# Odd layer's order at the heads' seams: k's rotation behind the output additions, y's transposes moved between products

## The reference

```python
def retention_mixer(h, pos, w_in, w_out):
    q, k, v, z = _split(h @ w_in, ODD_SPLITS)              # 4 heads: q, k 256 wide, v, z 512 wide
    q = xpos_rotate(q.reshape(qk_shape), pos)
    k = xpos_rotate(k.reshape(qk_shape), pos) * (RET_QK_DIM ** -0.5)
    v = v.reshape(bsz, s, RET_HEADS, RET_V_DIM)
    o = rms_norm(multiscale_retention(q, k, v)).reshape(bsz, s, ODD_MIX)
    return (jax.nn.silu(z) * o) @ w_out                    # y @ w_out, added to x
```

## Time and profile before

| | |
|---|---|
| median of 3 runs | 1869.29 us (1869.04 to 1871.68) |
| profiled execution | 1863.59 us, its span 1861.8 us |
| PE busy | 1779.9 us, 96% of the span |
| DVE, ACT, POOL busy | 657.0, 445.0, 239.3 us |
| mean granted clock of TensorE | 0.981 |

### The profile page before, as it was taken

How to read it: one execution, slowest core, us unless ns; L and a number is a source line. 1 busy time by engine, 2 the same in 40 slices (tenths; PEclk the granted TensorE clock), 3 DMA queues, 4 the chain that set the end, 5 groups by cost and what they waited for, 6 DMA issues and landing times. The chain is left out here.

```text
span 1861.8 us, 23173 instructions
## 1 busy us (share of the span) xinstructions
PE 1779.9 (96%) x9225; PEld 1131.5 (61%) x9225; DVE 657.0 (35%) x1141; ACT 445.0 (24%) x845; POOL 239.3 (13%) x154
## 2 busy tenths in 40 slices
PE   7999777999999999999999999999999999999998
PEld 7778776864545454544777877777854444545453
DVE  3666665343233332323413113130342323233333
ACT  4355535221111111111332132313321111111110
POOL 2521001100000000000243244234100000000000
PEclk9989898999999999999999999999999999999999
DMA  8310020279999999999122212122189999999996
GB/s 191 91 45 1 1 92 2 91 274 409 409 409 410 410 410 410 410 409 399 55 91 91 89 47 90 65 72 91 52 341 409 409 409 410 410 410 409 410 410 251
DMA packets 140953, 460.44 MB, mean 247 GB/s; under 512 B 5329, under 2 KB 31153, under 8 KB 139985
## 3 DMA queue, kind: packets, MB, share of 16 engines
q1 hardware_dynamic: 140080, 457.07, 63.2%
q0 software_dynamic: 800, 2.35, 1.0%
HBM read 457.30 MB, written 2.10 MB: 247 GB/s over the span
## 5 line engine op out<-in xcount | busy, mean ns | idle before, releaser
L1524 PE MATMUL bank<-ring,SCR 128*64 128x512 f32 x2048 | 448.3, 593 | 1.1 <-DVE SCR L1504 0.9
L153 PE MATMUL bank<-ring_r 128*128 128x512 f32 (+1 forms) x1152 | 355.2, 389 | 1.4 <-ACT SCR L507 1.4
L1524 PEld LDWEIGHTS bank<-ring,SCR 128*64 128x64 f32 x2048 | 152.7, 137 | 290.3 <-issue 284.9
L153 PEld LDWEIGHTS bank<-ring_r 128*128 128x128 f32 x1152 | 216.4, 190 | 47.4 <-issue 3.1
L1535 PE MATMUL bank<-ring,SCR 128*64 128x512 f32 x1024 | 226.8, 595 | 0.0
L1812 DVE TENSOR_TENSOR X<-X,bank 128x512 f32<-128x512 f32 x256 | 164.0, 681 | 99.7 <-PE bank L1542 99.3
L1962 POOL TENSOR_TENSOR ring_r<-ring,ring_r 128x1024 fp32r<-128x1024 f32 x60 | 145.0, 2449 | 253.0 <-ACT ring_r L1955 253.0
L1542 PE MATMUL bank<-SCR_r 128*128 128x512 f32 x512 | 153.4, 422 | 5.2 <-DVE SCR_r L1551 4.5
L1535 PEld LDWEIGHTS bank<-ring,SCR 128*64 128x64 f32 x1024 | 70.8, 137 | 132.1 <-issue 128.5
L1554 DVE SCALAR_TENSOR_TENSOR SCR<-SCR,bank 128x512 f32<-128x512 f32 x32 | 23.9, 748 | 359.4 <-PE bank L1524 359.4
L153 PE MATMUL bank<-ring_r,SCR_r 128*128 128x512 f32 x576 | 139.8, 401 | 10.2 <-DVE X L2167 10.2
(11 more groups left out here) (399 smaller groups left out, 1778.7 us busy)
## 6 DMA issues: line engine op xcount, KB each, us to landing
ring<-in_w_gate_dram SPq DMA_DIRECT2D x64, 2048.0 KB, 15.1
ring<-in_w_up_dram SPq DMA_DIRECT2D x64, 2048.0 KB, 18.4
ring<-in_w_down_dram SPq DMA_DIRECT2D x64, 2048.0 KB, 14.7
ring<-in_w_in_odd_dram SPq DMA_DIRECT2D x8, 2048.0 KB, 8.7
ring<-in_w_in_even_dram SPq DMA_DIRECT2D x16, 512.0 KB, 6.5
ring<-in_w_in_odd_dram SPq DMA_DIRECT2D x8, 1024.0 KB, 8.1
ring<-in_w_out_odd_dram SPq DMA_DIRECT2D x4, 2048.0 KB, 7.7
ring<-in_w_out_even_dram SPq DMA_DIRECT2D x2, 2048.0 KB, 10.4
```

What stands on the lines that cost most here:

```text
L153: mm = pe.matmul(out, lhs[a], rhs[b], start=(first and i == 0), stop=(last and i == 2))
L1524: mm = pe.matmul(bank[SLOTS * u:SLOTS * u + SLOTS, :], x_tile(k, u), w[u][:, k, :], start=(k == 0), stop=(k == KT - 1))
```

## The change

It touches the order of instructions on three engines, at the three seams. No instruction is added or removed.

```diff
--- before.py
+++ after.py
@@ -1967,10 +1967,12 @@
             left.append({"qk": ("r_qk", 2 * h + 2), "v": ("r_v", NT * (h + 1)), "z": ("r_z", NT * (h + 1)), "out": ("r_out", 8 * (h + 1))}[name])
         left = [(sg(a), b) for a, b in left]
 
-        def ret_qk_pe(pe, h):
+        def ret_qk_pe(pe, h, between=()):
             j, c, w = odd_chunk("qk", h)
             w = [a.rearrange("p (k s n) -> p k s n", k=KT, s=2) for a in w]
             for s in range(2):
+                for t in between if s else ():
+                    ret_yt_pe(pe, h - 1, t)
                 for par in range(2):
                     if h:
                         pe.wait_ge(sg("r_o_out"), NT * (h - 1) + 2 * s + par + 1)
@@ -2013,10 +2015,11 @@
                 if h < RH - 1:
                     for t in range(1, NT):
                         ret_z_pe(pe, h, t)
-                    ret_qk_pe(pe, h + 1)
-                    for t in range(NT):
-                        ret_yt_pe(pe, h, t)
+                    ret_qk_pe(pe, h + 1, (0, 1))
                     for n in range(8):
+                        if n == 2:
+                            ret_yt_pe(pe, h, 2)
+                            ret_yt_pe(pe, h, 3)
                         ret_out_pe(pe, h, n)
                 else:
                     ret_z_pe(pe, h, 1)
@@ -2104,8 +2107,8 @@
                     split_act(act, at("out", h))
                 for t in range(NT) if h < RH - 1 else range(1, NT):
                     yt_out(h, t)
-                if h < RH - 1:
-                    split_act(act, at("v", h + 1))
+                    if h < RH - 1 and t == 1:
+                        split_act(act, at("v", h + 1))
 
         def ret_pool(pool, step):
             at = lambda name, h: odd_at[name, h][0]
@@ -2155,12 +2158,13 @@
                         yt_lower(h, 0)
                 if h < RH - 1:
                     rotate(h + 1, both[0:1])
-                for t in range(NT) if h < RH - 1 else range(1, NT):
+                for t in range(2) if h < RH - 1 else range(1, NT):
                     yt_lower(h, t)
-                if h < RH - 1:
-                    rotate(h + 1, both[1:2])
                 for n in range(8):
                     t, half = n // 2, n % 2
+                    if h < RH - 1 and n == 2:
+                        yt_lower(h, 2)
+                        yt_lower(h, 3)
                     dve.wait_ge(sg("r_out"), 8 * h + n + 1)
                     xs = X[:, t, half * 512:(half + 1) * 512]
                     dve.wait_ge(resid, R_MOE0 + 8 * h)
@@ -2169,6 +2173,8 @@
                         if n == 1:
                             router_gain(dve, 1)
                         router_dve(dve, 1, n)
+                if h < RH - 1:
+                    rotate(h + 1, both[1:2])
 
 
         released = {c_kv: (sg("a_proj"), 4), c_q: (sg("a_proj"), 8)}
```

## The result

| | before | after |
|---|---|---|
| median | 1869.26 us (1869.04 to 1871.68, 4 runs) | 1850.49 us (1849.36 to 1853.49, 4 runs) |
| ratio | | 0.9908 [0.9893, 0.9924] |
| span of the profiled execution | 1861.8 us | 1847.5 us |

A forecast was written before the change was run, and what follows sets the result against it. TensorE was taken to bound the kernel, so time comes only from its waits and lower clock at three seams. 12.9 + 3.2 = 16.1 us gives 1847.5 us profiled, 1853.1 us for the median; range 1849.8 to 1858.4.

The forecast's parts named there:

- The two waits: At each seam TensorE idles 1.11 us for tile 0's lower part and 2.74 us for half tile 0's addition; both go.
- The seam's 12.9 us: From transposes to half tile 2's addition, 14.81 us against 10.52 of work: 4.29 us per seam, 12.9 over three.
- The clock's 3.2 us: Clock falls behind the first and third seams' idle time, 1.65 and 1.60 us, vanish with that idle time.
- k's rotation: Moved behind addition 7 on VectorE, it still ends before the next head's scores, with 14.7 us of slack.
- The copy of tile 2: On ScalarE behind four v casts taking 3.90 us, the copy still has some 2.1 us of slack.
- From the transposes of tile 2 to half tile 4: The 2.22 us chain of transpose, copy and difference is covered by transposes and products, with 4.3 us of slack.
- The remainder of the program moves up as a whole.: Second expert layer loads are released by TensorE's work behind the last seam, so everything after it starts earlier.
- rival 1: The waits go but the clock falls come elsewhere: gain 12.9 us, 1856.4 us; chance 0.14.
- the 5.7 us: Runs' median 1869.29 us lies this far above the profiled execution; it carries over, turning 1847.5 into 1853.1 us.
- Rival 2: The timed runs had a clock fall at all three seams: gain 17.8 us, 1851.5 us; chance 0.13.
- The port rule: Beside GpSimd the moved rotation stays slow, additions and differences are untouched; otherwise only 1.4 us of gain left.
- rival 4: Transpose-only stretches, two per seam, let the clock fall: six falls of 1.65 us, gain 6.2 us, 1863.1 us; chance 0.02.

The follow-up runs named there:

- e1: Kernel before with only k's rotation moved behind the additions on VectorE, transposes left together: ratio 0.9929 [0.9915, 0.9943].
- e2: Changed kernel with k's rotation put back ahead of the additions, so only transposes, copies and lower parts move: ratio 0.9931 [0.9917, 0.9944].
- e3: Kernel before plus ten useless products in TensorE's idle time ahead of half tile 2: median 1864.27 us against 1867.54, ratio 0.998.
- r1: Kernel before, unedited, run and profiled a second time: median 1867.51 us against 1867.54, ratio 0.9999 [0.999, 1.0008].
- e8: Changed kernel with nine useless casts ahead of v's casts on ScalarE: 1871.81 us in one execution, against 1866.52 for the kernel before.
- e5: Changed kernel with the four products of k's rotation done eleven times, rotation 29.0 us: median 1878.39 us, ratio 1.0063 against the kernel before.
- e4: Changed kernel with the four products of k's rotation done seven times, rotation 18.9 us: ratio 0.9902 [0.9887, 0.9917] against the kernel before.
- second pair: Second profiles of either kernel, both unedited: spans 1865.6 us before and 1848.2 us after.
- first pair: First profiles of the kernel before and the changed kernel: spans 1861.8 us and 1847.5 us.
- e6: Changed kernel with additions 0 and 1 ahead of tile 3's lower part in the last head: median 1845.89 us against the changed kernel's 1850.07, ratio 0.9887.
- first comparison: Kernel before against changed kernel, four runs each: medians 1869.26 and 1850.49 us, ratio 0.9908.
- r2: Changed kernel, unedited, run and profiled a second time: median 1850.07 us against 1867.16 for the kernel before, ratio 0.9906 [0.9893, 0.992].

## Why the prediction was right, point by point

**The two waits end, and nothing takes their place.** Right: the view of waits is empty over the seams. By e1 and e2 the waits were not two independent costs: either edit alone gives about two thirds of the whole. The prediction took the seam as a whole, from transposes to addition 2, and that is why its sum is right.

**The seam's 12.9 us.** Measured 107.14 − 102.66 = 4.48 us a seam, 13.4 in all. Two terms for the work that is left were off, in opposite directions. The 1.08 us for eight transposes had been read from transposes that started behind a wait; within running work they take 0.87 (1001.39 to 1002.26), so the work was put 0.42 us a seam too high. The changes between product and transposes were costed at nothing; the first matmul behind transposes takes 0.33 us instead of 0.23 (1002.26 to 1002.59), twice a seam, so the work was put 0.2 us too low. With both put right the forecast is 4.51 us a seam.

**The clock's 3.2 us.** Right in cause, and right in size for the profiled execution. The two falls cost 3.28 us by the marks (16.72 − 13.44), and e3, which has all the waits but fills one, gains 3.3. That equal waits may or may not bring a fall was right as well. Over all profiles of this study, by the length of TensorE's idle time in the odd layer's mixer:

| idle time | places | falls behind it |
|---|---|---|
| 1.1 us (transposes) | 12 (before, r1, e1, e3) | 0 |
| 1.4 us (e2) | 3 | 0 |
| 2.0 us (last head) | 11 | 7 |
| 2.7 us (before, r1) | 6 | 4 |
| 4.3 us (e8) | 3 | 3 |
| 7.9 us (e5) | 3 | 3 |

The length of one idle time does not settle it alone: in the router's work behind the mixer, where the longest is 0.93 us, 8 of the 12 profiles have a fall. What brings those was not tested.

**The slacks.** k's rotation: 14.7 us predicted, 14.6 measured (1043.48 to 1058.09), and e4 and e5 lie on the two sides of it. The copy of tile 2: 2.1 predicted, 1.97 measured. From the transposes of tile 2 to half tile 4: 4.3 predicted, and this step was wrong. It followed transpose, copy and lower part alone, and forgot that addition 2 is queued behind the lower parts of tiles 2 and 3 and frees the bank of half tile 4. In e8 the copies start at 1028.41 instead of 1020.75 (transposes' start and 0.67), 7.66 us late, and half tile 4 at 1030.96 instead of 1026.5, 4.5 us late: the slack is some 3.2 us. It cost nothing here.

**"The remainder of the program moves up as a whole."** Only nearly. In the second pair it does up to the expert loads (15.48 us at both marks). In the first pair 1.6 of the 16.4 us were lost again to a fall in the last head that the profile of before did not have, and 0.6 in the second expert layer. The cause of the 0.6 is open; from the first "up" load to the end the twelve profiles have 514.3 to 516.8 us, so it is within what that stretch varies by. This is the forecast's rival 1 in a small form: one fall of two came elsewhere. The new order is not needed for it, since e3 and r1, with the old order, have it too. The profile of e6, without the wait, has no fall there, but neither have four of the eleven with the wait, so e6 alone does not show that the wait is the cause.

**From the profile to the runs.** Forecast 16.1 us; the medians differ by 18.8 us in the first comparison and 17.1 in the second, and 16.7 lie in the seams in both pairs of profiles. The profiled executions differ by less, 1863.59 − 1849.41 = 14.2 us: the forecast's 1847.5 us for this execution was 1.9 us too low, and that the span came out at 1847.5 us is chance. The median is 2.6 us under the forecast's 1853.1. The forecast took the 5.7 us between the first profiled execution and the median as constant. It is spread: 21 runs of before lie between 1863.55 and 1870.01 us, and the first profiled execution lies at their low end. r1 shows most of such a difference (3.8 us) as falls of the clock outside the seams. That the 18.8 us are the 16.7 of the seams and some 2 us of chance in four runs against four is argued from this, not shown. Rival 2, a fall at all three seams in the timed runs, is not ruled out by it: 13.4 us of waits and three falls of 1.63 are 18.3 us. Take the waits that a kernel no longer has off the difference of its medians, and what is left for the clock is 5.3 us (first comparison), 3.7 (r2), 3.9 (e1), 4.0 (e2) and 3.3 (e3). In falls of 1.63 us these are 2.0 to 3.3, mostly between the forecast's two and the rival's three; single runs are too spread to say which.

**The port rule.** The Trainium skill ("SBUF — State Buffer", on the shared port pair) says that a VectorE instruction with two SBUF inputs contends with a GpSimd instruction that reads SBUF, and that one with at most one SBUF input, outside the modes that use two ports, does not. The traces agree: where k's rotation overlapped GpSimd with both its SBUF-only instructions (e2), both were slow (1.64 and 2.87 us, against 0.69 and 0.68 without GpSimd). In the changed kernel the additions at 1016.47 and 1019.20 took 0.69 us each within this stretch of GpSimd:

```profile
1014.93 9.49 POOL L1962 TENSOR_TENSOR ring_r<-ring,ring_r 128x1024 fp32r<-128x1024 f32 x4 [13.48 <-ACT ring_r L1955]
```

**The transposes and the clock (rival 4).** The clock was 1.00 through each of the 12 stretches of transposes in the seams of the two profiles of the changed kernel. The Trainium skill ("TensorE: Matmul & The Clock Gate", Part 4) says that the upper level of the clock does not engage in transpose mode; in stretches of eight transposes between products, as here, these traces do not show that.

## What to carry to other kernels

- When an engine waits twice in one stretch, time the stretch as a whole against the sum of its work. What two edits give need not add up: here 3.0 and 2.8 us a seam for either alone, 4.5 for both.
- A wait of the matmul engine can cost more than it shows, since the clock may fall behind it (1.6 us for each fall in the kernel before, up to 2.5 in e8); look at the granted clock behind every wait, and look for the next such wait when the first is gone (e6: 4 us more for one instruction moved behind two others, 2.25 of them the wait itself).
- Work whose result is wanted late (k's rotation, 14.6 us of slack) belongs behind work that frees a buffer for the bounding engine; to find its slack, follow every instruction queued behind it, not its own result alone.

## What had not been expected of the hardware

Eight transposes cost 0.87 us in running work and 1.08 behind a wait, and the first matmul after transposes 0.10 us more than the next. The same idle time of 2.0 us was followed by a fall of the clock in 7 of 11 profiles and one of 1.4 us in none of three places. In the one pair of profiles of the kernel before that was compared, such falls make up most of a difference of 3.8 us; that they make up most of the spread from run to run (6.5 us over 21 runs) is likely from this, not shown.
